# Projection stage of a diffusion backbone step: gate rows broadcast by DMA, q projected feature-major, sums on VectorE, gates on four column groups

## The reference, cut to what matters

```python
sh1, sc1, g1, sh2, sc2, g2 = split(silu(cvec) @ w_ada + b_ada, 6)   # for c_ctx and for c
h = rmsnorm(x, norm_mix) * (1 + sc1) + sh1
p = h @ w_in     # columns: q_m, k_m, v_m, o_m (512 each), 16 gates, q_d, k_d, v_d (512 each)
gates = p[gate columns] + b_gate        # 4 kinds (input, forget; both directions) x 4 heads
# mLSTM in chunks of 128 tokens, forward and backward, 4 heads of width 128:
b = cumsum(log_sigmoid(f));  dmat[l, s] = b[l] - b[s] + i[s]  (s <= l, else -inf)
m_t = max(b + m, max_s dmat);  s = (q k^T) * exp(dmat - m_t)
num = s v + exp(b + m - m_t) * (C q);   h_m = num / max(|den|, exp(-m_t))
C_new = decay * C + sum_s w_k v k^T
# beside it: differential attention, 4 heads, on q_d, k_d, v_d and cached keys and values
x = x + g1 * (concat(norm(h_m) * sigmoid(o_m), norm(h_d)) @ w_out)
x = x + g2 * moe(rmsnorm(x, norm_ffn) * (1 + sc2) + sh2)      # 16 experts, two per token
```

## Time and profile before

| | us |
|---|---|
| median of 3 runs | 817.06 |
| lowest, highest | 814.7, 818.93 |
| the profiled execution, its own time | 812.73 |
| its span (first to last instruction) | 811.0 |

### The profile page before, as it was taken

How to read it: one execution, slowest core, us unless ns; L and a number is a source line. 1 busy time by engine, 2 the same in 40 slices (tenths; PEclk the granted TensorE clock), 3 DMA queues, 4 the chain that set the end, 5 groups by cost and what they waited for, 6 DMA issues and landing times.

```text
span 811.0 us, 7471 instructions
## 1 busy us (share of the span) xinstructions
PE 696.1 (86%) x2640; PEld 354.5 (44%) x2640; DVE 320.5 (40%) x680; ACT 172.6 (21%) x407; POOL 108.3 (13%) x146
## 2 busy tenths in 40 slices
PE   3799999899999999997788989972499999999900
PEld 1443453335555555543566644541244444444400
DVE  2332262121443532456898254566120211112038
ACT  5000200001111111111567411211021111212133
POOL 1321000011010100002162200102200111110040
PEclk9999999999999999999899999995699999999955
DMA  8997413803030030303100377000289999999373
GB/s 293 386 355 234 144 64 115 301 1 117 18 113 0 2 116 0 104 0 108 49 1 1 131 256 288 27 26 27 77 286 347 360 369 349 366 340 348 133 269 145
DMA packets 58057, 135.18 MB, mean 167 GB/s; under 512 B 4962, under 2 KB 6202, under 8 KB 58028
## 3 DMA queue, kind: packets, MB, share of 16 engines
q1 hardware_dynamic: 46992, 107.08, 37.1%
q0 software_dynamic: 5632, 15.65, 5.4%
q10 hardware_dynamic: 5404, 12.06, 3.8%
HBM read 119.98 MB, written 14.76 MB: 166 GB/s over the span
## 4 chain that ended last, share of the span: by engine, by line
PE 76%; DVE 10%; DMA 5%; issue 4%; SPq 3%; ACT 2%; DVEq 0%; POOLq 0%; POOL 0%; ACTq 0%
PE PS L1326 29%; PE PS L1614 14%; PE PS L1527 8%; PE PS L1629 7%; DMA PR<-in_w_ada 3%; PE PS L1358 2%; PE PS L1581 1%; PE PS L1420 1%; PE PS L1414 1%; PE PS L1516 1%; DVE stat L1064 1%; DVE PR L936 1%; PE PS L1446 1%; PE PS L1607 1%; PE PS L1348 1%
## 5 line engine op out<-in xcount | busy, mean ns | idle before, releaser
L1326 PE MATMUL PS<-RING,hT 128*128 128x512 f32 x560 | 253.0, 599 | 1.3 <-DVE hT L895 1.3
L1326 PEld LDWEIGHTS PS<-RING,hT 128*128 128x128 f32 x560 | 102.6, 191 | 122.7 <-issue 121.8
L1614 PE MATMUL PS<-PR,RING 128*128 128x512 f32 x256 | 113.2, 595 | 0.1
L1527 PE MATMUL PS<-RING,hT 128*128 128x512 f32 x160 | 72.4, 608 | 0.0
L1614 PEld LDWEIGHTS PS<-PR,RING 128*128 128x128 f32 x256 | 47.4, 190 | 55.3 <-issue 53.6
L1629 PE MATMUL PS<-PR,RING 128*128 128x512 f32 x128 | 57.6, 592 | 0.0
L1527 PEld LDWEIGHTS PS<-RING,hT 128*128 128x128 f32 x160 | 30.3, 194 | 35.4 <-issue 35.3
L1206 DVE COPY RING<-PS 128x512 f32<-128x512 f32 x32 | 20.6, 687 | 55.5 <-PE PS L1607 54.9
L1211 DVE TENSOR_TENSOR RING<-RING,PS 128x256 f32<-128x256 f32 x16 | 6.8, 422 | 77.3 <-ACT RING L808 77.3
L1629 PEld LDWEIGHTS PS<-PR,RING 128*128 128x128 f32 x128 | 23.7, 190 | 26.8 <-issue 26.8
L1607 PE MATMUL PS<-ident,RING 128*128 128x128 f32 x128 | 18.6, 293 | 18.4 <-DMA RING<-scratch_h,idp 15.6
(11 more groups left out here) (289 smaller groups left out, 881.3 us busy)
## 6 DMA issues: line engine op xcount, KB each, us to landing
PR<-in_w_gate_up SPq DMA_DIRECT2D x16, 2048.0 KB, 10.1
PR<-in_w_ada SPq DMA_DIRECT2D x20, 1024.0 KB, 13.2
PR<-in_w_down SPq DMA_DIRECT2D x16, 1024.0 KB, 12.3
RING<-in_w_in SPq DMA_DIRECT2D x14, 1024.0 KB, 7.3
scratch_y<-RING ACTq DMA_DIRECT2D x16, 512.0 KB, 8.1
RING<-in_w_ada SPq DMA_DIRECT2D x4, 1024.0 KB, 13.1
RING<-in_w_out SPq DMA_DIRECT2D x4, 1024.0 KB, 6.8
scratch_h<-HM ACTq DMA_DIRECT2D x5, 512.0 KB, 2.6
```

Of the source, the lines that this page charges most:

```text
L1326: last = mm(PS[:, m % 2, :], hTv[:, k, t * P:(t + 1) * P], ring[:, ci % 2, k, :], start=(k == 0), stop=(k == KD - 1))
L1527: last = mm(PS[:, i % 4, :], hTv[:, k, t * P:(t + 1) * P], ring[:, (WOUT + q) % 2, k, :], start=(k == 0), stop=(k == KD - 1))
L1614: last = mm(PS[:, 4 + b, :], xgT[:, b, k, :], gub[b][:, k, :], start=(k == 0), stop=(k == KD - 1))
```

## The change

- `mqT` is projected feature-major: the mq weights of a head and a block k are the stationary operand and 512 columns of `hT` stream past. The 2560 columns (4 heads x 640 tokens) are cut into five units of 512; three of the units cover the end of one head and the start of the next, in two pieces. ScalarE writes them straight to `mqT`. Transposes and copies of mq go.
- The gates run in four column groups; VectorE adds four pieces.
- `ada2_sum` goes. VectorE adds the four groups, one after the other, onto the bias, which GpSimd now loads as two rows into the row buffer itself, after the row before it in that buffer has been stored. `ada2(n)` waits for row n-1 to be finished.
- The row of `gf` and the mask no longer come from TensorE. SyncE stores `gf` to DRAM (`scratch["gfr"]`) once the maxima are done, and for each step g loads 4 heads x 128 tokens, broadcast to 128 partitions, into `mbuf[g % 2]`. GpSimd adds the mask, ScalarE takes the exponentials from there. Buffer g waits for the exponentials of step g-2. The loads stand in SyncE's list behind chunk loads, as `MB_AFTER` says.
- Three semaphores of the gate chain are made one, `gate_step`, with the values 1 (min taken), 2 (maxima done), 3 (coefficients ready).

```diff
+    mbuf = TMP[:, 11796:12820].rearrange("p (b h t) -> p b h t", b=2, h=H)
+    mqT_flat = PR[:, 10260:12820]
-        if WIN_ORDER[m_ // NT] in ("mk", "mq", "dk", "dq"):
+        if WIN_ORDER[m_ // NT] in ("mk", "dk", "dq"):
             T_NO[m_] = len(T_NO)
+    MB_AFTER = {5: (0, 1), 6: (2, 3), 7: (4, 5, 6), 8: (7, 8, 9)}
+    def mq_spans(t_):
+        spans, lo = [], 512 * t_
+        while lo < 512 * (t_ + 1):
+            hi = min(512 * (t_ + 1), (lo // T + 1) * T)
+            spans.append((lo // T, lo % T, lo % T + hi - lo, lo - 512 * t_))
+            lo = hi
+        return spans
...
+        def load_mb(g):
+            d, t = MG[g]
+            if g == 0:
+                sp.wait_ge(gf_stored, 16)
+                sp.wait_ge(gate_step, 3)
+            if g >= 2:
+                sp.wait_ge(w_ready, g - 1)
+            src = scratch["gfr"][:, d * T + t * P:d * T + (t + 1) * P]
+            sp.dma_start(mbuf[:, g % 2], src.partition_broadcast(P)).then_inc(mb_in[g % 2], 16)
...
             if ci == 4:
                 load_ada2(8)
+                sp.wait_ge(gate_step, 2)
+                sp.dma_start(scratch["gfr"], gf.rearrange("p d t -> p (d t)")).then_inc(gf_stored, 16)
             if ci == 5:
                 for n_ in range(9, 12):
                     load_ada2(n_)
+            for g in MB_AFTER.get(ci, ()):
+                load_mb(g)
...
         def load_bias2(n_):
-            pool.dma_start(adp2[ROWS4 - 1:ROWS4, n_ % 2, :], bias[n_ * 512:(n_ + 1) * 512].unsqueeze(0)
+            pool.dma_start(ada_b2[n_ % 2], bias[n_ * 512:(n_ + 1) * 512].partition_broadcast(2)
                            ).then_inc(bias2_loaded[n_ % 2], 16)
...
+        pool.wait_ge(adacol_T, 4)
+        load_bias2(4)
+        load_bias2(5)
...
             pool.wait_ge(ada_row, n_ + 1)
-            if n_ >= 5:
-                pool.wait_ge(row_stored, 16 * (n_ - 4))
             pool.dma_start(scratch["mod"][:, (n_ - 4) * 512:(n_ - 3) * 512], ada_b2[n_ % 2]).then_inc(row_stored, 16)
+            pool.wait_ge(row_stored, 16 * (n_ - 3))
...
-            if g >= 1:
-                pool.wait_ge(mb_done, g)
-            nc.gpsimd.tensor_tensor(mdiag, gf[:, d, t * P:(t + 1) * P].unsqueeze(1).broadcast_to([H, H, P]),
-                                    eye4[:, 0, :].unsqueeze(2).broadcast_to([H, H, P]), ALU.mult).then_inc(mdiag_ready, 1)
+            pool.wait_ge(mb_in[g % 2], 16 * (g // 2 + 1))
+            nc.gpsimd.tensor_tensor(mbuf[:, g % 2], mbuf[:, g % 2], masks[:, d, :].unsqueeze(1).broadcast_to([P, H, P]),
+                                    ALU.add).then_inc(mb_ready, 1)
...
+            elif w == "mq":
+                nc.scalar.activation(mqT_flat[:, 512 * t:512 * (t + 1)], src, ACT.Copy).then_inc(mm_evac, 1)
...
-            act.wait_ge(mb_done, g + 1)
+            act.wait_ge(mb_ready, g + 1)
...
-                ins = nc.scalar.activation(wexp[:, g % 2, h, :], PS[:, 5, h * P:(h + 1) * P], ACT.Exp,
+                ins = nc.scalar.activation(wexp[:, g % 2, h, :], mbuf[:, g % 2, h, :], ACT.Exp,
...
             dve.wait_ge(ada_done, n_ + 1)
-            V.tensor_copy(adp2[0:ROWS4 - 1, n_ % 2, :], PS[0:ROWS4 - 1, 4, :]).then_inc(ada_part, 1)
-            dve.wait_ge(adacol_T, n_ + 1)
+            dve.wait_ge(bias2_loaded[n_ % 2], 16 * (n_ // 2 - 1))
             row = ada_b2[n_ % 2]
+            for g in range(3):
+                step(V.tensor_tensor(row, PS[32 * g:32 * g + 2, 4, :], row, ALU.add))
+            last = V.tensor_tensor(row, PS[96:98, 4, :], row, ALU.add)
...
-                    last = mm(PS[32 * (k % 2):32 * (k % 2) + 16, bank, 0:hi - lo], wgate[:, k, :], hTv[:, k, lo:hi],
-                              start=(k < 2), stop=(k >= KD - 2))
+                    g = 32 * (k % 4)
+                    last = mm(PS[g:g + 16, bank, 0:hi - lo], wgate[:, k, :], hTv[:, k, lo:hi], start=(k < 4), stop=(k >= 4),
+                              tile_position=(0, g))
...
+            if WIN_ORDER[c] == "mq":
+                spans = mq_spans(t)
+                ks = range(4 * hf, 4 * hf + 4) if len(spans) == 1 else range(KD)
+                for k in ks:
+                    h, lo, hi, o = spans[hf % len(spans)]
+                    last = mm(PS[:, m % 2, o:o + hi - lo], ring[:, ci % 2, k, h * P:(h + 1) * P], hTv[:, k, lo:hi],
+                              start=(k == 0), stop=(k == KD - 1))
+                if hf == 1:
+                    last.then_inc(mm_done, 1)
+                return
...
-            if n_ >= 5:
-                pe.wait_ge(ada_part, n_ - 4)
+            pe.wait_ge(ada_row, n_)
...
-            pe.wait_ge(mdiag_ready, g + 1)
-            if g >= 1:
-                pe.wait_ge(w_ready, g)
-            mm(PS[:, 5, :], identb[:], masksb[:, d, :].unsqueeze(1).broadcast_to([P, H, P]), start=True, stop=False)
-            mm(PS[:, 5, :], ones4[:], mdiag.rearrange("p h t -> p (h t)"), start=False, stop=True).then_inc(mb_done, 1)
```

More of the change, by code:

```diff
@@ L250, in build_body @@
     kw_ready = sem("kw_ready")
-    mdiag_ready = sem("mdiag_ready")
-    mb_done = sem("mb_done")
+    mb_in = [sem(f"mb_in{b}") for b in range(2)]
+    mb_ready = sem("mb_ready")
     int_done = sem("int_done")
@@ L272, in build_body @@
     sc_tail = sem("sc_tail")
-    ada_part = sem("ada_part")
+    gate_step = sem("gate_step")
+    gf_stored = sem("gf_stored")
     od_ready = sem("od_ready")
@@ L655, in win_out @@
             else:
-                rc = {"mq": 0, "dk": 1, "dq": 2}[w] * NT + t
+                rc = {"dk": 0, "dq": 1}[w] * NT + t
                 if rc >= 2:
                     act.wait_ge(win_T, NT + rc - 1)
-                if w != "mq" and t > 0:
+                if t > 0:
                     dst = xs[:, rc % 2].rearrange("p (g h j) -> p g h j", h=2, j=16)
@@ L669, in win_out @@
             if w == "mk" and t == NT - 1:
-                act.wait_ge(nabs_f, 1)
+                act.wait_ge(gate_step, 1)
                 step(nc.scalar.activation(ee, ee, ACT.Exp))
@@ L871, in ada_rows @@
             dve.wait_ge(ada_done, n_ + 1)
-            V.tensor_copy(adp2[0:ROWS4 - 1, n_ % 2, :], PS[0:ROWS4 - 1, 4, :]).then_inc(ada_part, 1)
-            dve.wait_ge(adacol_T, n_ + 1)
+            dve.wait_ge(bias2_loaded[n_ % 2], 16 * (n_ // 2 - 1))
             row = ada_b2[n_ % 2]
-            if n_ >= 6:
-                dve.wait_ge(row_stored, 16 * (n_ - 5))
+            for g in range(3):
+                step(V.tensor_tensor(row, PS[32 * g:32 * g + 2, 4, :], row, ALU.add))
+            last = V.tensor_tensor(row, PS[96:98, 4, :], row, ALU.add)
             if n_ in (8, 9):
-                last = V.scalar_tensor_tensor(row, PS[0:2, 5, :], 1.0, ada_g[:, (n_ - 8) * 512:(n_ - 7) * 512], ALU.add, ALU.mult)
-            else:
-                last = V.tensor_copy(row, PS[0:2, 5, :])
+                step(last)
+                last = V.scalar_tensor_tensor(row, row, 1.0, ada_g[:, (n_ - 8) * 512:(n_ - 7) * 512], ALU.add, ALU.mult)
             last.then_inc(ada_row, 1)
@@ L902, in _ @@
         dve.wait_ge(gate_done, 1)
-        step(V.tensor_scalar(grow, PS[0:16, 6:8, :].rearrange("p b n -> p (b n)")[:, 0:T], bgate[:], None, ALU.add))
-        V.tensor_tensor(grow, PS[32:48, 6:8, :].rearrange("p b n -> p (b n)")[:, 0:T], grow, ALU.add).then_inc(gate_rows, 1)
+        gsum = lambda g: PS[32 * g:32 * g + 16, 6:8, :].rearrange("p b n -> p (b n)")[:, 0:T]
+        step(V.tensor_scalar(grow, gsum(0), bgate[:], None, ALU.add))
+        step(V.tensor_tensor(grow, gsum(1), grow, ALU.add))
+        step(V.tensor_tensor(grow, gsum(2), grow, ALU.add))
+        V.tensor_tensor(grow, gsum(3), grow, ALU.add).then_inc(gate_rows, 1)
         dve.wait_ge(gate_split, 64)
         step(V.scalar_tensor_tensor(ee, gf, -1.0, gf, ALU.mult, ALU.min))
-        dve.sem_inc(nabs_f, 1)
-        DST = {"mk": mkT, "mq": mqT, "dk": dkT, "dq": dqT}
+        dve.sem_inc(gate_step, 1)
+        DST = {"mk": mkT, "dk": dkT, "dq": dqT}
         def win_evac(m):
@@ L1336, in heads_T @@
             if w in ("dk", "dq") and t > 0:
-                pe.wait_ge(roped, tn - (11 if w == "dk" else 12) + 1)
+                pe.wait_ge(roped, tn - (6 if w == "dk" else 7) + 1)
                 src = rr[:, (tn - NT) % 2]
@@ L1360, in ada2 @@
             last.then_inc(ada_done, 1)
-        def ada2_sum(n_):
-            pe.wait_ge(ada_part, n_ - 3)
-            pe.wait_ge(bias2_loaded[n_ % 2], 16 * (n_ // 2 - 1))
-            if n_ >= 5:
-                pe.wait_ge(ada_row, n_)
-            mm(PS[0:2, 5, :], misc[0:ROWS4, 40:42], adp2[:, n_ % 2, :], start=True, stop=True).then_inc(adacol_T, 1)
         for m in range(ALONE * NT):
@@ L1391, in _ @@
             if w == "mv" and t == 1:
-                pe.wait_ge(coef_args, 1)
+                pe.wait_ge(gate_step, 3)
                 for e in range(8):
@@ L1399, in _ @@
                 pe.wait_ge(cache_loaded, 32)
+                pe.wait_ge(ada_row, 12)
                 for h in range(H):
@@ L1644 @@
```

(3 more changed lines are left out.)

15 lines of the change are left out of this document (3 added, 12 removed).

## The result

| | us |
|---|---|
| changed kernel, median of 4 runs | 794.01 (792.03 to 794.49) |
| kernel before, median of 4 runs beside it | 816.25 (814.7 to 818.93) |
| ratio, 95% interval | 0.972 (0.9688 to 0.9752) |
| the profiled execution, its own time | 794.49 (span 792.8) |

The change gives 22.2 us by the medians (20.2 to 25.5 by the interval); forecast were 24.6 to 792.5, out of a sum of 23.9. The two profiled executions differ by only 18.2 us, and the profiled one, forecast at 788.8, took 794.49. Where these six go is the first thing to settle, since a sum that is checked against the wrong pair of numbers looks wrong.

The account below looks back on a forecast made before the run. TensorE's list was taken to bound the projection stage. Gains of 28.0 us less 0.2, 0.2, 2.0 and 1.7 gave 23.9, so a median of 793.2, stated as 792.5; own range 788 to 797, 8 in 10 784 to 802.

Parts of the forecast that it names:

- The bound: Projection stage: TensorE's list runs back to back, so a removed instruction saves its own time until something else is late.
- Gates: Gate passes on TensorE: four column groups instead of two take 2.3 us instead of 4.43, gain 2.1 us.
- Sums: Eight late modulation blocks: dropping the sum matmul inside a projection unit saves 1.15 us each, 9.2 us; VectorE's additions hidden.
- q: Projection of q: five transpose groups go, gain 2.2 us; shorter passes cost 0.2 us.
- the clock's term: Block 9's modulation product: half clock behind the longer stall, more likely than not, costing 1.7 us.
- Gate rows: Scan steps: two TensorE matmuls leave each of ten steps, 1.45 us each, gain 14.5 us; broadcasts cost 0.
- First row: Second modulation block's start: VectorE's additions for the first row just hidden, 0.2 us put as cost, bounds 0 and 1.
- The stall and the clock: Wait for block 9's weights: grows from 2.5 to about 4.4 us, giving back 2.0; likely half clock costs 1.7.
- rival (a): Stall before block 9's modulation: clock does not fall and nothing else is late, gain 26 us, 791; chance 0.25.
- Rival (c): Scan steps from the third: broadcasts exceed 27 us, TensorE waits at the value matmul, 24 us slower, 841; chance 0.05.

Follow-up runs that it names:

- e6: Kernel before with only the modulation sums moved to VectorE and the bias loads: 810.0 us, ratio 0.9922.
- e5: Kernel before with only q projected feature-major and copied directly to `mqT`: 816.22 us, ratio 0.9995.
- e7: Kernel before with only the gate rows broadcast by transfer: 802.75 us, ratio 0.9842.
- e11: Changed kernel with four useless products filling TensorE's wait for block 9's weights: 788.41 us, ratio to the kernel before 0.9667.
- e8: Changed kernel, each row from step 2 on requested only when that step's scores are done: 857.64 us, ratio to the kernel before 1.0491.
- e10: Changed kernel with rows requested that late, but GpSimd making `kw` ahead of the mask addition: 840.02 us, ratio to the kernel before 1.0287.
- e1: Kernel before, run again with no edit: 815.07 us, ratio 0.9999.
- e2: Changed kernel, run again with no edit: 791.65 us, ratio to the kernel before 0.9726.
- e3: Changed kernel with the gates back on two column groups: 793.97 us, ratio to the kernel before 0.9763.

## Why the prediction was right

- **The bound.** A list of TensorE pieces back to back, each removed piece worth its own length: right. Stage 24.4 against 23.9.
- **Gates.** 4.43 to 2.30, forecast 2.3; the factor of the modulation product (3.75) carried over, in spite of the second short piece of each k. By the Trainium skill's 3.07x for four row tiles (TensorE: Matmul & The Clock Gate, Measured speedup vs the span model) the gates would have taken 2.8 us, as an estimate: the trace differs, 4.43 x 1.94 / 2.30 = 3.7.
- **Sums.** Eight times 1.15 us, with nothing late on VectorE (the additions took 0.68 each). In e6: 6.35 = 9.2 less 1.2 given back and 1.66 of clock.
- **q.** 2.2 less 0.2, as forecast; two of five transposes given back. Alone it is worth nothing (e5), since the clock's term, which all parts share, then falls to it whole.
- **Gate rows.** 14.5 forecast, 14.7 in e7. That the broadcasts cost nothing was right, for the reason given (27 us or more ahead). The sizes were near: landing 5.0 us on the median (9.2 at most) where I took 6, GpSimd's addition 1.27 on the median where I took 1.1.
- **First row.** 0.2 forecast, 0 measured. "Just hidden" holds where the stage starts early: in e11 VectorE ends the additions at 67.44 and TensorE starts the second block at 67.83. In the first profile, with a later start, there are 4.4 us to spare (68.78 and 73.16).
- **The stall and the clock.** 2.5 to 4.4 us as worked out; the fall of the clock behind it was the likelier case and came in every profile with a wait of 3.3 us or more there, so rival (a) falls. Its price, 1.7, was 1.64. e11 shows that it is the idle time's. The reason I gave, the length of the wait, is only part of it: waits of 2.5 us elsewhere in the kernel came out both ways.
- **What I did not see** is that every profile carries a chance of 4 to 5 us in the front part. The profiled execution was forecast at 788.8 and took 794.49, 5.7 us more, 4.7 of them ahead of the stage and in its first unit. I noticed that the profiled run of before lay under all others and blamed nothing for it; the row was there (the earlier trace rows has the 16 passes at 3.56 us next to others at 1.90). The medians of the 4 runs average over it, which is why 792.5 was near; with four runs a side that is luck in part, as the medians differ by 22.2 us where the stage gave 24.4.
- **Rival (c)** had the right mechanism at the wrong place. I let it act on the value product, from a round trip of 27 us on; e8 and e10 show that a late row first stops the state update through GpSimd's list, then the state product through VectorE's. The point from which it decides is earlier than the one I wrote, and in the order chosen here `kw` is still 19 us ahead of its update in step 4, the tightest of those from step 2 on.

## What to carry to other kernels

Where one engine's list is full from end to end, add up what leaves the list, and then ask for each transfer that is requested from inside it how much work lies between request and use: what leaves there comes back as waiting, and may take the clock with it. A wait is to be priced by everything that stands behind the waiting instruction on its own engine, not only by the users of what it waits for. Before two profiles are compared, cut both at the same places; a part that the diff doesn't touch and that differs by microseconds is to be repeated before it is explained.

## What the runs showed of the hardware

- In the projection stage waits of TensorE of 2.5 us left its granted clock at 1.00 (before, e1, e7); waits of 3.3, 3.7 and 4.4 us were followed by half clock (e5, e6, the changed kernel, e2, e3). It lasted for the whole product behind them, 3.5 us instead of 1.90, except in e3, where it came later: 2.81 us for the product and 7.87 instead of 7.06 for the unit behind it. A wait of 0.94 us after 3.6 us of filler left it full (e11).
- At the output projection waits of 2.4 to 2.9 us came out both ways: half clock behind them in 10 of 14 profiles, full in e2, e3, e10 and e11.
- The two weight-bound products ahead of the projection ran at either level in different executions of the same kernel, moving the start of unit 0 between 40.05 and 45.15 us over 14 profiles.
- A broadcast of 4 x 512 bytes to 128 partitions (256 KB) landed in 5.0 us on the median (3.2 to 9.2; 4.0 in e8 and e10), about as long as a 256 KB load in longer rows (5.7).
